# The mixer's step order of a hybrid decoder block, written out as a table

## The chip, the cores and the metric

One core of one Trainium2 chip. The metric is the device time of one execution in microseconds (us), the median over the runs shown; lower is better. Engines: TensorE (PE; its weight loads are PEld), VectorE (DVE), ScalarE (ACT), GpSimd (POOL) and SyncE (SP), which issues the transfers here. Each engine works its own queue in order, and the engines meet only at semaphores.

## What is computed

A decoder block over 2048 tokens of width 1024, in float32, with three parts:

```python
proj = rmsnorm(x) @ w_in               # q, k, v, g, z and two conv halves
o_gla = rmsnorm(gla_chunked(q, k, v, log_sigmoid(z @ w_gate_up + b) / 16)) * silu(g)   # 4 heads
u = c_in * sigmoid(c_gate)             # then a causal depthwise conv of 31 taps, 512 channels
o_conv = silu(channel_group_norm(conv(u)))
h = x + concat(o_gla, o_conv) @ w_out
h = h + square(relu(rmsnorm(h) @ w_mlp_in)) @ w_mlp_out
out = rmsnorm(h)
```

Everything but the last two lines is called the mixer here, the rest the MLP. Both kernels compute the same.

## The kernel before

The mixer works in four blocks of 512 tokens (b = 0 to 3). Precise products are made of three passes (`three_products`, L69: high times high, high times low, low times high), so that a weight tile is split into a rounded high part by ScalarE (L968) and a low part by GpSimd (L832) when it is new, stored to `w_kept` and loaded from there for later blocks (L616). A weight step ("unit") is one such tile of 512 columns and 12 matmuls of 128x512. Four tiles are on chip at a time (`SLOTS`), so that a load waits until the unit four places back is used.

The steps of one block, as PE sees them: `z` (the low-rank gate input), `qk_a`/`qk` 0 to 3 (q and k; the `_a` is the first half of the sum), `gate` 0 and 1 (L1635), `v` 0 to 7, `g_a`/`g` 0 to 3, then four transposes `x_tr` of the next block's normed tokens (L1488), 16 `out` units (the output projection of the block before, L1699 to L1701, in two halves of eight), and `conv_gate`/`conv_in` 0 to 3 for the next block. Between them stand small steps of other parts:

- The GLA recurrence, per chunk c of 128 tokens: `gla_expo` (DVE, L1406 to L1408, 15 differences of the cumulated decay into `fac`), `gla_factors` (ACT, exponentials, L1145 to L1147), `gla_decayed` in three parts (POOL, products into `ke` and `qe`, L861 to L921), `gla_heads` (ACT, L1155), `gla_scores` in four parts (PE, L1742 and L1746), each followed by `gla_select` (DVE, two masked copies into `probs`, L1431 or L1422), and `gla_out` (PE L1766 to L1773, ACT copy L1168, DVE state update L1440). Part n+1 of the scores writes the bank that the select of part n reads, so PE waits for that select. All of a chunk's scores free what `gla_decayed` of the next chunk writes.
- `decay` (DVE, a scan, L1372) needs both `gate` steps and ScalarE's logarithm; `gla_expo` 0 needs `decay`.
- The depthwise convolution: 124 taps a block, each one DVE instruction of 128x512 (L1248), in two pairs of channel tiles with 62 taps each (`taps`, pair, first, count). A pair needs `conv_in` of its tiles (DVE product L1347, which also frees the bank for the next `conv_in_a`).
- `cn_mean`, `cn_var`, `cn_rstd`, `cn_silu`, `cn_mixed` norm the convolution's output, and `gn_square`, `gn_sum`, `gn_rstd`, `gn_mixed` that of the recurrence; `v_done` (ACT, L1125) empties the banks of `v`.
- `x_load`, `x_sq`, `x_norm` bring the next tokens; `res_load` (SP, L679), `out_done` (DVE, L1389) and `store` (SP) add the residual and write h.

One list, PROGRAM, holds all steps, and every engine runs through it and takes its own instructions (`run`). So the place of a step sets its order on each engine that has a part in it, SP's and POOL's queues too. Before, the list is made by a planner: `block_steps` lays down the PE steps in a fixed order and puts the others where a due time, counted in weight units, falls (`gla_events` and the tables `CN0`, `CN0_MIX`, `CN1`, `GLA_AT`); `add_taps` then puts so many taps ahead of each DVE step as the numbers of TAP_PLAN say, and completes a pair where `conv_in` or `cn_mean` needs it. `last_steps` writes the way into the MLP by hand: `x_tr` of b = 4, the four `up0` products, and the last 16 `out` units.

```python
    for step, b in steps:
        name = step[0]
        if on_dve(step, b):
            emit(plan.pop(0) if plan else 0)
```

The MLP (from about 890 us on) is a loop over 16 groups of 256 hidden columns for each half of the tokens and isn't touched.

Of the kernel before, what the change touches and what calls it, by code (L numbers as in the profile page):

```python
# [87 lines left out]
def take_units():

    unit = 0  # L90

    def take(name, arg, n):
        nonlocal unit
        unit += n
        return (name, arg, unit - n, n)

    def column(name, j):
        return [take(name + "_a", j, 1), take(name, j, 1)]

    return take, column  # L100


def gla_events(b):

    events = [(8, ("gla_expo", 0)), (9.5, ("gla_factors", 0))] + [(10 + 1.3 * i, ("gla_decayed", 0, i)) for i in range(3)]
    start, period = GLA_AT.get(b, (15.6, 7.4))
    for c in range(TT):
        o = start + period * c
        if c + 1 < TT:
            events += [(o + 0.1, ("gla_expo", c + 1))]  # L110
        events += [(max(o - 1, 16), ("gla_heads", c))]
        for part in range(PARTS):
            events += [(o + 0.8 + PART_GAP * part, ("gla_scores", c, part)), (o + 0.8 + PART_GAP * part, ("gla_select", c, part))]
        if c + 1 < TT:
            events += [(o + 1.6, ("gla_factors", c + 1))]
            events += [(o + 2.6 + 1.2 * i, ("gla_decayed", c + 1, i)) for i in range(3)]
        events += [(o + 0.8 + PART_GAP * PARTS + 0.4, ("gla_out", c))]
    o = events[-1][0]
    if b < NB - 1:
        events += [(o + 1, ("gn_square",)), (o + 2.6, ("gn_sum", 0)), (o + 3.6, ("gn_sum", 1)), (o + 4.6, ("gn_rstd",))]  # L120
    return [(u, e, b) for u, e in events]


def block_steps(b, over):

    mix, nxt = b > 0, b < NB - 1
    kind = "start" if not mix else "body" if nxt else "end"
    take, column = take_units()
    steps = [] if nxt else [(("g2_load",), b)]
    steps += [(("x_load", t), b) for t in range(2 if mix else TT)]  # L130
    steps += [] if nxt else [(("m_load", i), b) for i in range(FT)]
    head = [("z",), *column("qk", 0), ("gate", 0), *column("qk", 1), ("gate", 1), *column("qk", 2),
            ("decay",), *column("qk", 3)]
    fill = head + [take("v", k, 1) for k in range(KT)]
    fill += [("v_done", 2 * 4 + KT - 1)]
    fill += [s for h in range(HEADS) for s in column("g", h)]
    fill += [("x_tr", 0), ("x_load", 2), ("x_tr", 1), ("x_load", 3)] if mix else [("x_tr", 0), ("x_tr", 1)]
    if mix:
        out0 = [take("out", (0, k), 1) for k in range(KT)]
        fill += out0[:1] + [("res_load", 0)] + out0[1:] + [("out_done", 0, out0[-1][2])]  # L140
    fill += [("x_tr", 2), ("x_tr", 3)]
    if mix:
        out1 = [take("out", (1, k), 1) for k in range(KT)]
        fill += [] if nxt else [("next_x", 0), ("next_x", 1)]
        fill += out1[:2] + [("store", 0)] + out1[2:3] + [("res_load", 1)] + out1[3:] + [("out_done", 1, out1[-1][2]), ("store", 1)]
    if nxt:
        for j in range(CT):
            fill += column("conv_gate", j) + column("conv_in", j)

    ev = over + gla_events(b)  # L150
    if mix:
        ev += [(0.8, ("cn_rstd", 1), b - 1), (1.6, ("cn_silu", 1), b - 1), (3.0, ("cn_mixed", 1), b - 1)]
        ev += [((13.2 + 1.2 * h if b == 1 else 4 + 1.4 * h), ("gn_mixed", h), b - 1) for h in range(HEADS)]
    ev += [(8 + i, ("x_sq", i), b) for i in range(2)] + [(12 + i, ("x_norm", i), b) for i in range(2)]
    late, scale = (26.6, 29) if mix else (12, 16)
    ev += [(late + i, ("x_sq", 2 + i), b) for i in range(2)] + [(scale + i, ("x_norm", 2 + i), b) for i in range(2)]
    if not nxt:
        ev += [(34.5 + i, ("x_sq", i), b + 1) for i in range(2)] + [(36.5 + i, ("x_norm", i), b + 1) for i in range(2)]
        ev += [(38 + 1.4 * i, ("m_split", i), b) for i in range(FT)]
    ev += [((20 if b == 1 else CN0[kind]) + u, (n, 0), b) for u, n in zip((0, 1.8, 3.3), ("cn_mean", "cn_var", "cn_rstd"))]  # L160
    ev += [(CN0[kind] + 8, ("cn_silu", 0), b), (CN0_MIX[kind], ("cn_mixed", 0), b)]
    if nxt:
        ev += [(CN1[kind] + u, (n, 1), b) for u, n in zip((0, 1.8), ("cn_mean", "cn_var"))]
    ev.sort(key=lambda e: e[0])

    at = 0
    for f in fill:
        while ev and len(f) == 4 and ev[0][0] <= at:
            steps.append(ev.pop(0)[1:])
        steps.append((("x_load", f[1]), b + 1) if f[0] == "next_x" else (f, b))  # L170
        if len(f) == 4:
            at += f[3]
    return steps, [(u - at, *e) for u, *e in ev]


CN0 = {"start": 28.5, "body": 17.5, "end": 17.5}
CN0_MIX = {"start": 38, "body": 40.2, "end": 40.2}
CN1 = {"start": 36.5, "body": 52.5}


def first_steps():

    s = []
    take, column = take_units()
    for j in range(CT):
        s += [(f, -1) for f in column("conv_gate", j) + column("conv_in", j)]
        s += [(("make_wz",), -1)] if j == 1 else []
    return s


def last_steps():

    take, column = take_units()
    out = [[(take("out", (half, k), 1), NB) for k in range(KT)] for half in range(2)]
    gla, mlp = NB - 1, NB

    def at(b, *steps):
        return [(step, b) for step in steps]

    s = at(gla, ("gn_square",)) + at(mlp, ("x_tr", 0), ("x_load", 2)) + at(gla, ("up0", 0), ("gn_sum", 0))  # L200
    s += at(mlp, ("x_tr", 1), ("x_load", 3)) + at(gla, ("gn_sum", 1), ("gn_rstd",), ("up0", 1))
    s += at(mlp, ("x_sq", 2)) + at(gla, ("cn_mean", 1)) + at(mlp, ("x_norm", 2), ("x_tr", 2), ("x_sq", 3))
    s += at(gla, ("cn_var", 1), ("gn_mixed", 0), ("gn_mixed", 1)) + at(mlp, ("x_norm", 3), ("x_tr", 3))
    s += at(gla, ("m_load", 2), ("m_load", 3), ("cn_rstd", 1), ("gn_mixed", 2), ("gn_mixed", 3), ("up0", 2))
# [7 lines left out]

def mixer_steps():

    steps, over = first_steps(), []
    for b in range(NB):
        more, over = block_steps(b, over)
        steps += more
# [1623 lines left out]
```

## Time and profile before

| | |
|---|---|
| median of 3 runs | 2349.61 us (2348.43 to 2351.4) |
| the profiled execution | 2348.33 us, of which its trace spans 2346.3 us |
| busy, share of the span | PE 96%, PEld 78%, DVE 51%, ACT 31%, POOL 28% |
| mean granted TensorE clock | 0.984 of full |
| the chain of waits, by engine | PE 74%, DVE 10%, POOL 2%, issue 1%, ACT 1%, DMA 1% |

A busy share is an average over stages: PE is at work without a break in the MLP, while in the mixer it waits now and then. The chain of waits goes back from the last instruction to what released it, and where it runs through DVE or POOL, that engine set the pace.

### The profile page before, as it was taken

How to read it: one execution, taken by the hardware profiler on the slowest of the kernel's cores; microseconds unless marked ns; L12 is line 12 of the kernel's file. 1: busy time of each engine (PE TensorE's matmuls, PEld its weight loads, DVE VectorE, ACT ScalarE, POOL GpSimd, SP SyncE). 2: the span in 40 equal slices, each digit the busy share in tenths (PEclk: the TensorE clock that was granted, in tenths of full speed). 3: DMA queues.
4: the chain of work that ended last, by engine and by line, in shares of the span. 5: the costliest groups of instructions: out<-in, count | busy, mean ns of one | idle time of the engine just before them, and what ended most of it. 6: DMA issues, size and time to landing. Idle time of an engine off the chain costs nothing.

```text
span 2346.3 us, 27675 instructions
## 1 busy us (share of the span) xinstructions
PE 2242.8 (96%) x10192; PEld 1831.6 (78%) x10192; DVE 1198.6 (51%) x1949; ACT 720.2 (31%) x1014; POOL 664.9 (28%) x697
## 2 busy tenths in 40 slices
PE   7989978998999999999999999999899999999998
PEld 6768767776877777888888888887788888888887
DVE  2898974389439942343433333436433343343345
ACT  3444553345235543112212212224221221221222
POOL 6443345142304332212221221224221222122122
...
GB/s 253 248 166 126 149 167 137 211 179 135 169 178 183 153 189 152 188 46 54 49 40 54 54 39 50 54 82 62 197 46 44 54 52 37 54 54 44 46 36 72
DMA packets 148518, 252.24 MB, mean 108 GB/s; under 512 B 9792, under 2 KB 91744, under 8 KB 148448
## 3 DMA queue, kind: packets, MB, share of 16 engines
...
## 4 chain that ended last, share of the span: by engine, by line
PE 74%; DVE 10%; POOL 2%; issue 1%; ACT 1%; DMA 1%; POOLq 0%; SPq 0%; ACTq 0%
PE acc L71 11%; PE acc L73 11%; PE acc L72 11%; PE acc L1566 10%; PE acc L1568 10%; PE acc L1567 10%; DVE acc L1248 5%; PE acc L1699 2%; PE acc L1701 2%; PE acc L1700 2%; PE acc L1742 2%; DVE fac L1406 1%; DVE fac L1407 1%; PE acc L1488 1%; PE acc L1718 1%
## 5 line engine op out<-in xcount | busy, mean ns | idle before, releaser
L1308 DVE TENSOR_TENSOR h_sb<-acc,h_sb 128x512 f32<-128x512 f32 x512 | 350.0, 690 | 274.8 <-PE acc L1568 268.4
L1566 PE MATMUL acc<-dn_hi,ff_hi 128*128 128x512 f32 x1024 | 400.1, 391 | 7.3 <-DVE h_sb L1308 5.5
L1567 PE MATMUL acc<-dn_lo,ff_hi 128*128 128x512 f32 x1024 | 399.1, 390 | 0.0
L1568 PE MATMUL acc<-dn_hi,ff_lo 128*128 128x512 f32 x1024 | 399.1, 390 | 0.0
L1326 DVE TENSOR_TENSOR relu<-relu 128x512 f32<-128x512 f32 x124 | 85.8, 692 | 463.4 <-ACT relu L1048 463.4
L884 POOL TENSOR_TENSOR up_lo<-raw_a,up_hi 128x1024 fp32r<-128x1024 f32 x62 | 149.3, 2431 | 584.5 <-ACT up_hi L1022 584.5
L1248 DVE SCALAR_TENSOR_TENSOR acc<-u_sb,cw_col,acc 128x512 f32<-128x512 f32 x464 | 312.0, 748 | 0.1
L884 POOL TENSOR_TENSOR dn_lo<-raw_b,dn_hi 128x1024 fp32r<-128x1024 f32 x62 | 147.2, 2396 | 456.0 <-ACT dn_hi L1022 456.0
L1566 PEld LDWEIGHTS acc<-dn_hi,ff_hi 128*128 128x128 f32 x1024 | 192.8, 188 | 47.9 <-DVE h_sb L1308 5.9
L1022 ACT ACTIVATE dn_hi<-raw_b 128x1024 fp32r<-128x1024 f32 x62 | 62.3, 1051 | 527.6 <-PE acc L1568 527.6
L1568 PEld LDWEIGHTS acc<-dn_hi,ff_lo 128*128 128x128 f32 x1024 | 192.7, 188 | 40.1
L1567 PEld LDWEIGHTS acc<-dn_lo,ff_hi 128*128 128x128 f32 x1024 | 192.8, 188 | 39.8
L71 PE MATMUL acc<-xT_hi,wt 128*128 128x512 f32 x512 | 213.8, 418 | 7.5 <-ACT v_sb L1125 4.7
L71 PE MATMUL acc<-xT_hi,up_hi 128*128 128x512 f32 x512 | 199.8, 390 | 3.2 <-DVE hT_lo L1280 3.2
L71 PE MATMUL acc<-hT_hi,up_hi 128*128 128x512 f32 x512 | 200.1, 391 | 1.5 <-DVE hT_lo L1267 1.5
L72 PE MATMUL acc<-xT_lo,wt 128*128 128x512 f32 x512 | 201.3, 393 | 0.0
L73 PE MATMUL acc<-xT_hi,wt 128*128 128x512 f32 x512 | 201.3, 393 | 0.0
L1048 ACT ACTIVATE relu<-acc 128x512 f32<-128x512 f32 x124 | 74.1, 598 | 413.3 <-PE acc L73 413.3
L73 PE MATMUL acc<-hT_hi,up_lo 128*128 128x512 f32 x512 | 199.9, 390 | 0.0
L72 PE MATMUL acc<-hT_lo,up_hi 128*128 128x512 f32 x512 | 199.9, 390 | 0.0
L72 PE MATMUL acc<-xT_lo,up_hi 128*128 128x512 f32 x512 | 199.2, 389 | 0.0
L73 PE MATMUL acc<-xT_hi,up_lo 128*128 128x512 f32 x512 | 199.2, 389 | 0.0
...
## 6 DMA issues: line engine op xcount, KB each, us to landing
wt<-w_kept SPq DMA_DIRECT2D x168, 512.0 KB, 3.3
raw_a<-in_w_mlp_in SPq DMA_DIRECT2D x64, 512.0 KB, 4.3
raw_b<-in_w_mlp_out SPq DMA_DIRECT2D x62, 512.0 KB, 3.5
w_kept<-wt SPq DMA_DIRECT2D x56, 512.0 KB, 4.9
...
h_sb<-h_dram SPq DMA_DIRECT2D x16, 512.0 KB, 8.9
out_h<-h_sb SPq DMA_DIRECT2D x16, 512.0 KB, 2.6
...
```

Source lines behind the costliest of these rows:

```text
L71: nc.tensor.matmul(out, w_hi, x_hi, start=first, stop=False)
L72: nc.tensor.matmul(out, w_hi, x_lo, start=False, stop=False)
L73: return nc.tensor.matmul(out, w_lo, x_hi, start=False, stop=last)
L884: nc.gpsimd.tensor_tensor(m_lo[i], raw[i], m_hi[i].bitcast(F32), ALU.subtract).then_inc(m_lo_ok, 1)
L1022: nc.scalar.activation(m_hi[i], raw[i], ACT.Copy).then_inc(m_hi_ok, 1)
L1048: nc.scalar.activation(relu[:, i, :], ps[:, i, :], ACT.Relu).then_inc(relu_ok, 1)
L1248: nc.vector.scalar_tensor_tensor(out=y_sb[:, j, :] if k == TAPS - 1 else bank, in0=u_sb[:, j, k:k + BLK], scalar=cw_col[:, j, k:k + 1], in ...
L1308: nc.vector.tensor_tensor(h_tile[t][:, c], ps[:, 4 + n % 4, :], h_tile[t][:, c], ALU.add).then_inc(add_ok, 1)
L1326: nc.vector.tensor_tensor(relu[:, i, :], relu[:, i, :], relu[:, i, :], ALU.mult).then_inc(sqr_ok, 1)
L1566: nc.tensor.matmul(o, ff_hi[:, i, r], m_hi[FT + i][:, c], start=(i == 0), stop=False)
L1567: nc.tensor.matmul(o, ff_hi[:, i, r], m_lo[FT + i][:, c], start=False, stop=False)
L1568: ins = nc.tensor.matmul(o, ff_lo[:, i, r], m_hi[FT + i][:, c], start=False, stop=(i == FT - 1))
```

## The change

PROGRAM is no longer planned. A literal table, ORDER, lists block, name and arguments of each step, taps included, and `mixer_steps` only numbers the weight units. The planner's functions and tables go. What an engine does in a step, the semaphores, the banks and the tiles are as before, and so are the order of the weight units and every step but the taps in number and kind (the 496 taps are cut into other groups, 755 entries before and 759 after).

```diff
-DVE_STEPS = (...)
-PART_GAP = 1.1
-GLA_AT = {0: (15.6, 6.9), NB - 1: (15.6, 6.6)}
-def take_units(): ...
-def gla_events(b): ...
-def block_steps(b, over): ...
-CN0 = ...
-def first_steps(): ...
-def last_steps(): ...
-def on_dve(step, b): ...
-def add_taps(steps): ...
-TAP_PLAN = [...]
+ORDER = [
...
+    (-1, "conv_gate", 1), (-1, "conv_in_a", 1), (0, "taps", 0, 0, 1), (-1, "conv_in", 1), (-1, "conv_gate_a", 2),
+    (-1, "conv_gate", 2), (0, "taps", 0, 1, 15), (-1, "make_wz"), (0, "x_load", 0), (-1, "conv_in_a", 2),
...
+    (0, "taps", 0, 16, 17), (-1, "conv_in", 3), (0, "z"), (0, "qk_a", 0), (0, "qk", 0), (0, "taps", 0, 33, 11),
...
+    (0, "x_sq", 2), (0, "v", 4), (0, "v_done", 15), (0, "gla_heads", 0), (0, "gla_decayed", 0, 2), (0, "x_sq", 3),
...
+    (1, "gla_decayed", 0, 2), (1, "gla_factors", 0), (1, "v", 6), (1, "gla_heads", 0), (0, "gn_mixed", 0),
...
+    (1, "gla_expo", 2), (1, "g", 2), (1, "g_a", 3), (1, "g", 3), (1, "x_tr", 0), (1, "gla_scores", 1, 0),
+    (1, "taps", 1, 55, 1), (1, "x_tr", 1), (1, "gla_select", 1, 0), (1, "x_load", 2), (1, "gla_select", 1, 1),
+    (1, "gla_select", 1, 2), (1, "x_load", 3), (1, "res_load", 0), (1, "out", 0, 0), (1, "cn_rstd", 0),
+    (1, "gla_scores", 1, 1), (1, "out", 0, 1), (1, "gla_decayed", 2, 0), (1, "gla_factors", 2),
+    (1, "gla_scores", 1, 2), (1, "gla_scores", 1, 3), (1, "x_sq", 2), (1, "x_sq", 3), (1, "gla_select", 1, 3),
...
+    (1, "out_done", 0, 31), (1, "gla_decayed", 2, 2), (1, "out", 0, 5), (1, "out", 0, 6), (1, "gla_heads", 2),
...
+    (1, "gla_select", 2, 1), (1, "gla_expo", 3), (1, "out", 1, 2), (1, "gla_scores", 2, 3), (1, "out", 1, 3),
...
+    (1, "conv_in", 1), (1, "conv_gate_a", 2), (2, "taps", 0, 0, 14), (1, "gn_rstd"), (1, "conv_gate", 2),
+    (1, "cn_var", 1), (2, "x_load", 0), (1, "conv_in_a", 2), (2, "taps", 0, 14, 3), (1, "conv_in", 2),
+    (1, "conv_gate_a", 3), (1, "conv_gate", 3), (1, "cn_rstd", 1), (1, "conv_in_a", 3), (1, "cn_silu", 1),
+    (2, "taps", 0, 17, 14), (1, "conv_in", 3), (2, "z"), (2, "qk_a", 0), (2, "qk", 0), (1, "gn_mixed", 0),
...
+    (2, "conv_in_a", 2), (3, "m_load", 0), (3, "taps", 0, 1, 28), (2, "conv_in", 2), (2, "cn_var", 1),
...
+    (3, "gn_square"), (4, "x_sq", 2), (3, "m_load", 2), (3, "m_split", 1), (3, "m_load", 3), (4, "x_norm", 2),
...
+]
 def mixer_steps():
+    steps, units = [], {}
+    for b, name, *args in ORDER:
+        if name in WEIGHT_STEPS:
+            n = units.get(b, 0)
+            units[b] = n + 1
+            steps.append(((name, args[0] if len(args) == 1 else tuple(args), n, 1), b))
+        else:
+            steps.append(((name, *args), b))
+    return steps
...
-        PROGRAM = add_taps(mixer_steps())
+        PROGRAM = mixer_steps()
```

Taps of a block that stand ahead of the last `conv_in` that feeds it, from there to `gla_expo` 0, and from there to the first `gla_select`, counted in both lists:

| block | taps ahead of `conv_in` 3, before / after | from it to `gla_expo` 0 | from it to `gla_select` 0, 0 |
|---|---|---|---|
| 0 | 2 / 33 | 48 / 25 | 77 / 49 |
| 1 | 30 / 32 | 46 / 41 | 74 / 64 |
| 2 | 6 / 31 | 40 / 22 | 63 / 48 |
| 3 | 6 / 33 | 40 / 17 | 63 / 41 |

In block 1, `gla_expo` 2 stood between the two first `x_tr` and `gla_select` 1, 0 and `gla_expo` 3 right ahead of `out_done` 0; now they stand ahead of `x_tr` 0 and behind `gla_select` 2, 1.

## Rows read from the trace of the kernel before

**Rows 1.** The page, first part: busy time of PE and its weight loads.
```profile
PE 2242.8 (96%) x10192; PEld 1831.6 (78%) x10192; DVE 1198.6 (51%) x1949; ACT 720.2 (31%) x1014; POOL 664.9 (28%) x697
```

**Rows 2.** Windows by stage: width, then each engine's busy time, granted clock, DMA share.
```profile
22.60:234.70 212.10, 198.53 (x933) 159.03 (x934) 160.34 (x297) 93.41 (x134) 100.71 (x141) 0.98 0.59 198
234.70:477.00 242.30, 216.21 (x1029) 172.52 (x1028) 147.22 (x266) 106.28 (x149) 80.86 (x112) 0.95 0.49 165
477.00:697.00 220.00, 207.00 (x983) 165.54 (x982) 151.37 (x279) 89.41 (x120) 60.62 (x96) 0.96 0.49 163
697.00:859.00 162.00, 151.86 (x778) 122.85 (x777) 142.67 (x259) 75.37 (x102) 65.50 (x104) 0.99 0.56 189
859.00:905.00 46.00, 40.22 (x157) 29.44 (x156) 20.84 (x30) 31.79 (x50) 12.83 (x14) 0.89 0.19 69
905.00:2346.30 1441.30, 1421.06 (x6289) 1175.96 (x6287) 565.03 (x809) 311.42 (x439) 333.06 (x198) 1.00 0.21 67
```

**Rows 3.** Waits of PE, 22 to 905 us: total us, times, longest.
```profile
PE acc L1742 <- DVE probs L1431: 22.5, 7, 5.2
PE acc L1488 <- DVE res_sb L1389: 13.8, 2, 10.2
PE acc L71 <- ACT v_sb L1125: 4.7, 1, 4.7
...
PE acc L1657 <- ACT k_sb L1115: 3.5, 4, 2.1
```

**Rows 4.** Windows around the start of block 2, same columns.
```profile
434.00:477.00 43.00, 43.00 (x190) 32.92 (x189) 11.82 (x22) 17.11 (x24) 0.00 (x0) 1.00 0.47 155
477.00:540.00 63.00, 57.47 (x249) 43.93 (x248) 62.79 (x109) 33.45 (x44) 27.10 (x35) 0.98 0.53 176
```

**Rows 5.** Timeline of DVE, block 2: start, us, engine, line, operation.
```profile
477.74 10.62 DVE L1248 SCALAR_TENSOR_TENSOR acc<-u_sb,cw_col,acc 128x512 f32<-128x512 f32 x16
...
505.40 5.77 DVE L1372 TENSOR_TENSOR_SCAN cum<-cum,sig 128x128 f32<-128x128 f32 x8
...
538.62 0.91 DVE L1431 COPY_PREDICATED probs<-lvl_mask,acc 128x256 f32<-128x256 int32 x2
```

**Rows 6.** Timeline of PE, block 2, at the second part of the scores.
```profile
539.58 1.65 PE L1742 MATMUL acc<-qe_head,ke 128*128 128x128 f32 x6 [4.04 <-DVE probs L1431]
```

**Rows 7.** Timeline of PE, block 0: matmuls of 512 columns at two paces.
```profile
127.32 0.63 PE L73 MATMUL acc<-xT_hi,wt 128*128 128x512 f32 x1
127.75 0.63 PE L71 MATMUL acc<-xT_hi,wt 128*128 128x512 f32 x1
...
134.67 0.40 PE L71 MATMUL acc<-xT_hi,wt 128*128 128x512 f32 x1
134.90 0.39 PE L72 MATMUL acc<-xT_lo,wt 128*128 128x512 f32 x1
```

**Rows 8.** Timeline of ACT, block 0: a weight split, later the heads.
```profile
125.14 0.63 ACT L968 ACTIVATE wt<-w_raw 128x512 fp32r<-128x512 f32 x1 [3.07 <-DMA w_raw<-in_w_in]
...
127.58 1.92 ACT L1155 ACTIVATE qe_head<-qe 64x896 f32<-64x896 f32 x2
```

**Rows 9.** Timeline of DVE, block 1: `gla_expo` 3 and `out_done` 0.
```profile
376.64 1.33 DVE L1406 TENSOR_TENSOR fac<-cum 128x128 f32<-128x128 f32 x1 [2.23 <-POOL qe L921]
...
379.17 0.28 DVE L1406 TENSOR_TENSOR fac<-cum 128x128 f32<-128x128 f32 x1
379.37 1.34 DVE L1407 TENSOR_TENSOR fac<-cum 128x128 f32<-128x128 f32 x1
...
384.17 2.48 DVE L1389 TENSOR_TENSOR res_sb<-acc,res_sb 128x512 f32<-128x512 f32 x4
```

**Rows 10.** Timeline of PE, block 1, at `x_tr` 2.
```profile
385.61 1.73 PE L1488 MATMUL acc<-ident,x_nat 128*128 128x128 f32 x7 [10.23 <-DVE res_sb L1389]
```

**Rows 11.** DMA issues: size of each, median us from issue to landing.
```profile
wt<-w_kept SPq DMA_DIRECT2D x168, 512.0 KB, 3.3
```

**Rows 12.** Timeline of POOL, block 1, beside rows 9.
```profile
379.29 1.28 POOL L832 TENSOR_TENSOR wt<-w_raw,wt 128x512 fp32r<-128x512 f32 x1 [0.19 <-ACT wt L968]
```

More of the change, by code:

```diff
@@ L81 @@
 WEIGHT_STEPS = COLUMNS + COLUMN_HALVES + ("v", "out")
-DVE_STEPS = ("make_wz", "conv_in", "gate", "decay", "gla_expo", "gla_select", "gla_out", "x_norm", "x_tr", "out_done",
-             "cn_mean", "gn_rstd", "cn_rstd", "cn_mixed", "ff0")
-PART_GAP = 1.1
-GLA_AT = {0: (15.6, 6.9), NB - 1: (15.6, 6.6)}
[L88 to L100, printed above, removed]
@@ L103, in gla_events @@
[L103 to L121, printed above, removed]
@@ L124, in block_steps @@
[L124 to L173, printed above, removed]
@@ L176 @@
[L176 to L204, printed above, removed]
-    s += at(gla, ("cn_silu", 1), ("cn_mixed", 1), ("up0", 3)) + at(mlp, ("res_load", 0))
-    s += out[0][:2] + at(gla, ("ff0", 0), ("ff0", 1)) + out[0][2:4] + at(mlp, ("res_load", 1))
-    s += at(gla, ("ff0", 2), ("ff0", 3)) + out[0][4:6] + at(gla, ("m_split", 2), ("m_split", 3)) + out[0][6:]
-    s += at(mlp, ("out_done", 0, out[0][-1][0][2])) + out[1][:4] + at(mlp, ("store", 0), ("late_load",)) + out[1][4:]
-    s += at(mlp, ("out_done", 1, out[1][-1][0][2]), ("store", 1))
-    return s
@@ L213, in mixer_steps @@
-def mixer_steps():
[L215 to L218, printed above, removed]
-    return steps + [tuple(e) for _, *e in over] + last_steps()
-def on_dve(step, b):
-    name = step[0]
-    if name in ("cn_rstd", "cn_mixed"):
-        return b == NB - 1 and step[1] == 1
-    return name in DVE_STEPS
-def add_taps(steps):
-    out = []
-    todo = [(m, p, i) for m in range(NB) for p in range(2) for i in range(PAIR_TAPS)]
-    plan = list(TAP_PLAN)
-    def emit(n):
-        while n > 0:
-            m, p, i = todo[0]
-            k = min(n, PAIR_TAPS - i)
-            out.append((("taps", p, i, k), m))
-            del todo[:k]
-            n -= k
-    for step, b in steps:
-        name = step[0]
-        if on_dve(step, b):
-            emit(plan.pop(0) if plan else 0)
-        if name == "conv_in" and b >= 0:
-            emit(sum(1 for m, p, i in todo if m < b or m == b and p <= step[1] // 2))
-        if name == "cn_mean":
-            emit(sum(1 for m, p, i in todo if m < b or m == b and p <= step[1]))
-        out.append((step, b))
-    assert not todo
-    return out
```

130 lines of the change are left out of this document (128 added, 2 removed), and 7 rows, old and new, of the table TAP_PLAN.

## Prediction

> **What bounds the kernel.** I read the busy shares first: PE is at work for 2242.8 of 2346.3 us, so all that any order can win is 103.5 us of idle PE, and a little clock [rows 1]. The windows by stage say where that is. After 905 us the loop runs, which the change doesn't touch. The mixer's stages are idle for width less busy: 13.6, 26.1, 13.0, 10.1 and 5.8 us, 68.6 in all [rows 2]. The first 22.6 us are startup and stay. The waits of PE name the releasers: 22.5 us for VectorE's selects, 13.8 for its residual sums, 4.7 for the copy of v, 3.5 for that of k [rows 3]. VectorE has only half its time filled, so the order matters: in 434 to 477 us it works 11.8 of 43 us while PE is full, and in the next 63 us it works all but 0.2 and PE loses 5.5 [rows 4].
>
> **Prices.** A tap costs 10.62/16 = 0.664 us in a run of taps, `decay` 5.8, a select pair 0.9 [rows 5]. Twelve matmuls, 0.227 us apart at full clock (134.67 to 134.90), make 2.7 us a weight unit [rows 7]. The profiled execution took 2348.3 us, 1.3 under the median of 2349.6; savings come off both.
>
> **Clock.** After a stall, matmuls start 0.43 us apart instead of 0.23, thus at 1.2 instead of 2.4 GHz [rows 7]. I count some 50 of them in six stretches behind stalls from 126 to 892 us: 50 x 0.2 = 10 us, of which 2.4 in block 0, 4.0 in block 1, 1.6 in block 2, 2 at the end. The Trainium skill (TensorE: Matmul & The Clock Gate, Terms) prices a throttled clock at its time times the share of pulses withheld; with the granted clocks of the stages that would be 32 us, and a kernel without the stalls would come out some 12 us lower than my sum. Most of that lower clock lies inside the idle time, which is counted already, so I keep 10.
>
> **Part 1: taps go where VectorE was idle.** 33, 32, 31 and 33 taps stand ahead of `conv_in` 3 instead of 2, 30, 6 and 6, and the path to `gla_select` 0, 0 holds 28, 10, 15 and 22 fewer. In block 2 VectorE runs without a break from 477.7 to the select at 538.6, and PE waits 4.04 us for it [rows 5, 6]; 15 taps less are 10.0 us, so that stall goes, and its twins in blocks 0, 1 and 3 (22 taps, 14.6 us) too. The next to be late is the chain `gla_factors`, `gla_decayed`, `gla_heads`; it hangs on `gla_expo` 0, which comes earlier by 23, 5, 18 and 23 taps, so it isn't late in blocks 2 and 3. Price of the new places: PE waits at `conv_in_a` and `qk_a` for VectorE's product behind the taps. Block 2: 14 taps (9.3) stand against two units and the 16 matmuls of `z` (2 x 2.7 + 3.6 = 9.0), nothing worth a term. Block 3: 28 taps (18.6) and two products, each taken as a select (1.8), 20.4 us, against six units (16.3) and six matmuls of the norms (some 3.3) on PE, 19.6: 0.8 us. Where GpSimd or a late start holds VectorE up, this cover is gone and each microsecond counts in full; the ends are 0 and 5 a block, for 14 taps are nearly two units of work more than there is room for if VectorE is late by one.
>
> **Part 2: block 1's second half.** `gla_expo` 3 waited for GpSimd until 376.6 and took until 384.2, `out_done` behind it; `x_tr` 2 stood 10.23 us [rows 9, 10]. With it behind `gla_select` 2, 1, `out_done` starts on its `out_pe` and the stall goes. With `gla_expo` 2 ahead of `x_tr` 0, so does a stall of 5.2 at the scores, one of the seven [rows 3]. What remains: `gla_scores` 1, 2 and 1, 3 now stand side by side, as do 3, 0 and 3, 1, and each pair makes PE wait for a select, 0.9 plus handover, 1.4 each. `x_norm`, `x_load`, the stores: bounded by nothing and 1 us; I take nothing, since the same transfers run under the same units.
>
> **Part 3: block 0.** `v_done` moves ahead of the splits of `v` 5 to 7 on ScalarE; before, a split waited 3.07 us for a load, and the copy of v behind it cost PE 4.7 [rows 3, 8]. Now the first scores come ahead of `g_a`, and wait for `gla_heads`: the last copy of v, taken as the split's 0.63, and the heads' 1.92 behind `v` 7 make 2.6 us, where POOL's `gla_decayed` is ready by then; if it is not, up to 5 [rows 8]. The `xT_lo` and select stalls go with the taps.
>
> **Part 4: SP's queue.** `res_load` 0 stands ahead of `out` 0, 0 (block 1) and of `g_a` 2 (block 2), and waits there for GpSimd's `cn_rstd`; weight loads queue behind it. A load has three units, 8.2 us, before it is needed, and lands in 3.3 [rows 11]: 4.9 us of slack. I find a delay of about 3. Cost 0, bound 0 to 5 for each of three blocks. GpSimd's splits behind `gla_decayed` 3, 0 get through 1 to 2 us ahead of PE by the same count.
>
> **Part 5: the way into the MLP.** `m_split` 1 now stands behind `x_sq` 2, which waits for a load, and `gn_sum` 1 behind both: 2.4 us new. `x_tr` 2 no longer waits, 2.0 less. The others stay. I take 0, between -3 and +5.
>
> **Sum**, idle and slow clock, before to after:
>
> - block 0: 13.6 + 2.4 to 5.4 (2.6 heads, 1.0 clock, 1.8 small): 10.6
> - block 1: 26.1 + 4.0 to 9.4 (2.0 k copy and 1.6 clock stay, 1.5 `out` and gate, 2.8 score pairs, 1.5 small): 20.7
> - block 2: 13.0 + 1.6 to 3.5 (a pair 1.4, `x_tr` 0.5, selects 1.6): 11.1
> - block 3: 10.1 to 5.5 (1.8 at `gla_out` stays, `conv_in_a` 0.8, selects 2.9): 4.6
> - end: 5.8 + 2 to the same: 0
>
> Together 47.0. A count on paper finds the waits that it looks for; the before has 26 stalls in 68.6 us, 2.6 each, and I put in three that I don't see: 7.9. That leaves 39.1, and 2349.6 - 39.1 = 2310.5; I say 2311. Nothing removed could give more than 68.6 + 10 = 78.6, thus 2271.
>
> **Rivals.** *Half of it* (0.17): blocks 0 and 1, where GpSimd also splits new weights, turn their stalls into others of the same size, and only blocks 2 and 3 gain: 11.1 + 4.6 = 15.7, 2334. For it: `gate` 0 of block 1 sits behind 24 taps and a `gla_out`, and PE is then held by `gate_min`. Against it: block 1 loses its two largest stalls whatever the taps do.
>
> *Nothing* (0.08): each stall is replaced, within 0.2% (4.7 us, about what a measurement here can tell from no change). The 26 stalls would have to be replaced by as much; 2350. For it: a step can only be early on one engine by being late for another. Against it: VectorE has 31 us of the 43 free where the taps go [rows 4].
>
> *Slower, the shared access to memory* (0.11). `gla_expo`'s differences take 0.28 us, but 1.34 while GpSimd subtracts [rows 9, 12]; a whole `gla_expo` with four of them took 7.5 us (376.64 to 384.17) against 14 x 0.2 + 0.4 = 3.2. The new places put `gla_expo` 0 and 1 beside `gn_mixed` and `gla_decayed`. If half of the 16, on the path, are stretched by 4.3, that is 34 us, and what part 1 gains (about 32 of the 47) goes too, so 2350 - 15 + 34 = 2369. It decides once a block's stretch passes the 10 us by which its selects come earlier. Against it: GpSimd is busy for 28% of the span only [rows 1], and the new places of `gla_expo` 2 and 3 take these two out of GpSimd's splits. The Trainium skill (SBUF — State Buffer, Who interferes with whom) states that a VectorE instruction with two SBUF inputs is shut out by a GpSimd instruction that reads SBUF, and that one with a single SBUF input isn't; by that rule the taps, one of whose inputs is in PSUM, never stretch. The trace agrees for both kinds.
>
> That the change does nothing can't be: the order of most small steps differs.
>
> **Numbers.** The forecast holds with 0.64, from 2290 (all but 19 us of the 78.6) to 2328. *Half of it* carries the range up to 2340; that leaves out the other two. Faster 0.81, same 0.08, slower 0.11.
>
> **What would show it.** In the profile after: VectorE busy some 20 us more in the 43 us ahead of the last `conv_in` of blocks 2 and 3; no PE wait over 2 us for `probs`; none for `res_sb` at `x_tr` 2; a new wait for `qe_head` of 2 to 3 us in block 0, and of 1.4 us at three pairs of scores; the loop's 1441 us unchanged. I am wrong if PE waits for `u_sb` in the conv stage by more than 3 us a block, for `wt` loads, or for the heads in blocks 1 to 3.

## The result and the profile after

The changed kernel takes **2277.82 us** (median of 4 runs, 2274.8 to 2278.47) against 2349.02 for the one before beside it (4 runs): a ratio of 0.9694, 95% interval 0.9677 to 0.9711, thus 71.2 us or 3% faster. The prediction said faster, but 2311, with a range from 2290 to 2340. The direction is right, but the measured time lies 33 us below the forecast and 12 us below the range.

The page after, first part:

```profile
PE 2225.5 (98%) x10192; PEld 1820.1 (80%) x10192; DVE 1186.5 (52%) x1949; ACT 713.8 (31%) x1011; POOL 660.7 (29%) x697
```

Beside [rows 1]: the same 10192 matmuls, and PE is not only idle for 52.7 us less (50.8 of 2276.3 instead of 103.5), it is also *busy* for 17.3 us less. DVE has the same 1949 instructions and is busy for 12.1 us less. Two engines do the same work faster, which an order alone doesn't seem able to do; both differences are explained below.

Windows of after, cut at the fourth `u_sb` product of each block (the `conv_in` 3 of the prediction) and at the first matmul of the MLP; columns as in [rows 2]:

```profile
22.60:70.62 48.02, 48.02 (x203) 38.72 (x204) 26.53 (x41) 14.69 (x24) 30.57 (x40) 1.00 0.86 295
70.62:223.55 152.93, 148.70 (x740) 119.84 (x738) 136.80 (x257) 74.61 (x105) 66.56 (x99) 0.99 0.56 188
223.55:436.54 212.99, 209.65 (x1032) 166.35 (x1031) 153.70 (x289) 115.55 (x162) 89.21 (x118) 1.00 0.55 187
436.54:636.13 199.59, 198.04 (x974) 159.34 (x973) 148.69 (x280) 82.23 (x114) 54.88 (x94) 1.00 0.53 181
636.13:816.06 179.93, 171.98 (x866) 137.50 (x865) 135.56 (x250) 91.41 (x130) 67.14 (x111) 0.99 0.51 174
816.06:2276.30 1460.24, 1441.29 (x6352) 1192.09 (x6352) 574.14 (x820) 322.80 (x457) 341.12 (x204) 0.99 0.21 67
```

The same for before, where its windows in [rows 2] ended elsewhere:

```profile
696.94:888.28 191.34, 175.42 (x869) 138.66 (x867) 156.49 (x277) 96.21 (x134) 72.81 (x114) 0.98 0.51 171
888.28:2346.30 1458.02, 1437.78 (x6352) 1189.62 (x6352) 572.10 (x820) 322.37 (x457) 338.59 (x203) 1.00 0.21 67
```

The mixer ends at 816.06 instead of 888.28, 72.2 us earlier; what follows is untouched and takes 2.2 us longer. Of the 72.2, 51.5 are idle PE (68.6 to 17.1, width less busy over the mixer's windows) and 20.7 are PE's busy time.

PE's waits after, 22 to 860 us (total us, times, longest), to be held against [rows 3]:

```profile
PE acc L1715 <- DVE probs L1404: 3.4, 3, 1.3
PE acc L1461 <- DVE x_nat L1229: 2.5, 2, 1.4
PE acc L1715 <- ACT qe_head L1128: 2.5, 1, 2.5
PE acc L1739 <- DVE probs L1395: 2.4, 3, 1.7
```

The selects went from 22.5 us to 3.4, the residual sum (13.8) and the copy of v (4.7) from the list altogether.

### The profile page after: what moved, and what is told of

It is laid out like the page before. It is cut to its first block, busy times and chain, and to the rows that moved or that the text cites. A ratio compares the mean times of both kernels' runs of the same rounds, so it can differ in the third digit from the quotient of the medians.

```text
span 2276.3 us, 27673 instructions
## 1 busy us (share of the span) xinstructions
PE 2225.5 (98%) x10192; PEld 1820.1 (80%) x10192; DVE 1186.5 (52%) x1949; ACT 713.8 (31%) x1011; POOL 660.7 (29%) x697
## 4 chain that ended last, share of the span: by engine, by line
PE 92%; DVE 5%; ACT 2%; issue 1%; DMA 0%; POOL 0%; SPq 0%; POOLq 0%; ACTq 0%
PE acc L71 15%; PE acc L72 15%; PE acc L73 15%; PE acc L1539 10%; PE acc L1540 10%; PE acc L1541 10%; PE acc L1672 2%; PE acc L1674 2%; PE acc L1673 2%; PE acc L1715 2%; PE acc L1630 1%; PE acc L1632 1%; PE acc L1631 1%; DVE acc L1221 1%; PE acc L1461 1%; PE acc L1739 1%
## 5 line engine op out<-in xcount | busy, mean ns | idle before, releaser
L73 PE MATMUL acc<-xT_hi,wt 128*128 128x512 f32 x512 | 200.9, 392 | 0.0
```

What stands on the lines that cost most here:

```text
L73: return nc.tensor.matmul(out, w_lo, x_hi, start=False, stop=last)
```

## The experiments

All kernels are written as a literal table like the new one, so "the order of before" is what the planner gave, put down as a table. Here are the mixer's stages of each run's trace, cut as above (width, and in brackets the idle PE in it), and the median. Each kernel was timed beside the kernel before, whose own median lay between 2346.5 and 2349.0. The intervals stand with each run and are ratios to that kernel. Where a run is held against the new table's 2277.8, two measurements at different times are compared, so differences of 2 or 3 us there say nothing. The trace is of one execution; that of `decay_back` took 2299.5 us, 7 us more than its median, which its readings below have to bear.

| kernel | start and block 0 | block 1 | block 2 | block 3 and way into the MLP | median |
|---|---|---|---|---|---|
| before | 212.1 (13.6) | 242.4 (26.1) | 219.8 (13.0) | 191.3 (15.9) | 2349.0 |
| taps_only | 219.2 (17.0) | 237.6 (23.0) | 227.9 (19.6) | 201.9 (20.3) | 2371.9 |
| steps_only | 219.0 (17.8) | 224.7 (12.7) | 208.9 (5.7) | 205.9 (28.8) | 2344.0 |
| taps_decay | 216.3 (13.6) | 238.1 (21.5) | 217.4 (13.0) | 192.8 (17.6) | 2346.1 |
| gn_only | 212.4 (13.5) | 238.3 (22.5) | 210.4 (7.2) | 187.9 (11.8) | 2332.3 |
| named4 | 214.2 (13.8) | 228.8 (14.2) | 216.6 (11.8) | 192.0 (15.4) | 2334.9 |
| named4_conv | 202.3 (5.5) | 229.4 (15.0) | 207.8 (6.3) | 189.6 (16.0) | 2311.9 |
| after | 200.9 (4.2) | 213.0 (3.3) | 199.6 (1.6) | 179.9 (8.0) | 2277.8 |

**The two halves of the change.** `taps_only` takes the order of before and puts every tap ahead of the VectorE step that it has behind it in the new table; `steps_only` is the reverse. In block 2, as an example:

```diff
 (2, "qk", 0),
-(2, "taps", 0, 6, 16), (2, "gate", 0), (2, "qk_a", 1), (2, "qk", 1), (2, "taps", 0, 22, 9), (2, "gate", 1),
+(2, "taps", 0, 31, 14), (2, "gate", 0), (2, "qk_a", 1), (2, "qk", 1), (2, "taps", 0, 45, 1), (2, "gate", 1),
 (2, "qk_a", 2), (2, "qk", 2),
-(2, "taps", 0, 31, 15), (2, "decay"),
+(2, "taps", 0, 46, 5), (2, "decay"),
```

> The order of before with every tap moved to where the new table has it (ahead of the same VectorE step); all other steps stay. The prediction put some 32 of its 47 us down to the taps. Theory A (a stall costs its idle time, and matmuls of 512 columns at half rate are all that the clock adds): 2349 less about 32, thus near 2317, and PE's busy time falls by no more than 6 us. Theory B (the lower clock behind each stall reaches the narrow matmuls too and costs some 0.4 us for each us of idle time): near 2304, with PE's busy time down by 12 or more. Rival C (taps alone change nothing without the steps, since gla_expo still comes late): 2335 or more.

> The new table's order of all other steps, with the taps ahead of the same VectorE steps as before the change (10 taps deferred to the conv_in that they need, 16 of block 3 drawn ahead of a cn_mean). If the two parts add up, as the prediction's sum takes them to, its gain and that of the run with the taps alone make 71 us together; theory A gives 15 us of them here, 2334; theory B 22, 2327. If the gains need each other, the two together stay clearly below 71 us; if they overlap, they come out above it.

The taps alone are **slower**: 2371.9 us, ratio 1.0095 (1.0070 to 1.0119). The steps alone give almost nothing: 2344.0, 0.9982 (0.9969 to 0.9996). 24 us lost and 4 won make 71 won when put together. This refutes the prediction's view that 32 of the 47 us belong to the taps, and theories A and B. Rival C had the reason, and its 2335 or more holds, but it spoke of no change, not of 24 us lost. (One wait of 11.3 us for `y_sb` in block 3 of `steps_only` comes from 16 taps that this mixture has to put ahead of a `cn_mean`. The steps alone are thus judged too low here: without that wait they would win some 15 us, an estimate from 4.1 + 11.3 that wasn't tested. Even so the halves don't add up to 71.)

The trace of `taps_only` says why. VectorE in block 2, ahead of the scan `decay`, and ScalarE at the same time, then ScalarE's logarithm in the same block of the kernel before:

```profile
496.75 3.38 DVE L1218 SCALAR_TENSOR_TENSOR acc<-u_sb,cw_col,acc 128x512 f32<-128x512 f32 x5
506.49 5.82 DVE L1342 TENSOR_TENSOR_SCAN cum<-cum,sig 128x128 f32<-128x128 f32 x8 [6.36 <-ACT sig L1077]
```

```profile
501.02 0.60 ACT L1085 ACTIVATE k_sb<-acc 128x512 f32<-128x512 f32 x1 [4.97 <-PE acc L73]
501.64 1.28 ACT L1075 ACT_TABLE_LOAD   x1
502.93 1.06 ACT L1075 ACTIVATE sig<-sig 128x1024 f32<-128x1024 f32 x1
504.01 1.28 ACT L1077 ACT_TABLE_LOAD   x1
505.30 1.15 ACT L1077 ACTIVATE sig<-sig,one_col 128x1024 f32<-128x1024 f32 x1
```

```profile
504.00 1.15 ACT L1107 ACTIVATE sig<-sig,one_col 128x1024 f32<-128x1024 f32 x1
```

VectorE has done its taps at 500.1 and waits 6.4 us for ScalarE's logarithm. ScalarE was free for five of them, but the step `decay` stands behind `qk` 2, and so its logarithm behind the copy of the result of `qk` 2, which PE has only then. The scan begins at 506.5, 1.1 us later than before [rows 5], in a block whose fourth `u_sb` product begins 2.3 us later (479.4 against 477.1). So it comes 1.2 us earlier in its block, where 20 taps less on the way from there to it would have made 13. Before, the taps had only filled this wait: the logarithm ended at 505.15 and the scan began at 505.40. The taps taken away ahead of it bought next to no time, and 9 instead of 3 now stand right ahead of the select: the wait at the scores grew from 4.0 to 8.2 us.

**decay.** One step moved per block, in the old order and in the new one:

```diff
+(2, "decay"),
 (2, "qk_a", 2), (2, "qk", 2),
-(2, "decay"),
```

> The run with the taps alone, and the step decay of each block ahead of the next weight unit where the new table has it (before qk_a 2, in block 1 before qk 2), two units earlier. Theory D: with the taps alone VectorE idles 6.4 us in block 2 ahead of decay, because ScalarE's logarithm for it stands in ScalarE's queue behind the copies of qk 2; so gla_expo 0 is no earlier than before, and the taps moved behind it make the select late. With decay moved this idle goes in every block, the waits for the selects of chunk 0 (8.2 and 5.5 us in blocks 2 and 3) shrink to under 3 us, and the time falls from 2372 to 2350 or below. Rival E (decay isn't what is missing, the other steps are): less than 8 us come back, 2364 or more.

> The new table with decay alone moved back behind qk 2 in all four blocks. Theory D: VectorE waits some 6 us for the logarithm in each block, and the selects of chunk 0 get late by what slack doesn't take: 15 to 30 us in all, so 2293 to 2308, most of it in blocks 2 and 3. Rival E: the slack of the new order covers it, and the time is within 5 us of 2278.

With `decay` two units earlier (one in block 1), the taps' run falls from 2371.9 to 2346.1, 0.9985 (0.9975 to 0.9996), and the waits in blocks 2 and 3 from 8.2 and 5.6 to 2.1 and 2.4, as theory D had it. Moved back in the new table, the step costs 14.5 us: 2292.3, 0.9758 (0.9742 to 0.9775), somewhat below the 15 to 30 expected, and in its trace, whose mixer is 21.2 us wider, more in blocks 0 and 1 (7.6 and 5.2 us) than in 2 and 3 (4.7 and 3.8), against what was expected. What PE waits for there is ScalarE's copy of k, which now stands behind the logarithm and its two table loads. PE in blocks 0 and 1, and ScalarE in block 0:

```profile
101.54 0.50 PE L1630 MATMUL acc<-wt,xT_hi 128*128 128x512 f32 x1 [2.93 <-ACT k_sb L1088]
270.51 0.79 PE L1630 MATMUL acc<-wt,xT_hi 128*128 128x512 f32 x1 [3.16 <-ACT k_sb L1088]
```

```profile
95.15 1.28 ACT L1078 ACT_TABLE_LOAD   x1
96.44 1.06 ACT L1078 ACTIVATE sig<-sig 128x1024 f32<-128x1024 f32 x1
97.52 1.28 ACT L1080 ACT_TABLE_LOAD   x1
98.82 1.15 ACT L1080 ACTIVATE sig<-sig,one_col 128x1024 f32<-128x1024 f32 x1
...
100.91 0.57 ACT L1088 ACTIVATE k_sb<-acc 128x512 f32<-128x512 f32 x1
```

The same place thus costs in two ways: late for VectorE, and late for PE.

**gla_expo 2 and 3 of block 1.**

```diff
+(1, "gla_expo", 2),
 (1, "g", 2), (1, "g_a", 3), (1, "g", 3), (1, "x_tr", 0), (1, "x_load", 2), (1, "x_tr", 1), (1, "x_load", 3),
-(1, "gla_expo", 2),
...
-(1, "gla_expo", 3),
 (1, "out", 0, 7), (1, "out_done", 0, 31),
...
 (1, "gla_scores", 2, 1), (1, "gla_select", 2, 1),
+(1, "gla_expo", 3),
```

> The order of before with two moves in block 1: gla_expo 2 ahead of g 2, and gla_expo 3 behind gla_select 2, 1. Two stalls of PE, of 10.2 and 5.2 us, should go. Theory A: 15.4 us less or somewhat under it, so 2334 to 2337. Theory B: the clock comes back with them, 15.4 x 1.4 = 21.6, so near 2328, with PE's busy time 4 us or more below before's. Rival: the select or the residual sum stays late by its taps, and less than 10 us come back.

> The new table with gla_expo 2 and 3 of block 1 moved back to where they stood (ahead of gla_select 1, 0 and of out_done 0). If the prediction's part 2 is right, the stall at x_tr 2 returns with about 10 us and that at the scores with up to 5: idle 15, with the clock's 0.4 for each 21, thus 2293 to 2299. If the two moves are worth in the new order what they were in the old one (11.5 us measured), 2289. If the new order no longer has GpSimd in their way, less than 5 us, 2283.

Alone the two moves give 11 to 12 us: 2336.6, 0.9947 (0.9929 to 0.9965). Both stalls go (0.5 us is left of the 10.2), but PE now comes to `out` 1, 0 before VectorE has taken the low half of the transposed tokens out of the banks that this unit writes:

```profile
377.37 0.80 PE L1671 MATMUL acc<-wt,mix_hi 128*128 128x512 f32 x1 [3.46 <-DVE xT_lo L1239]
```

Taken back from the new table they cost 8.5: 2286.3, 0.9735 (0.9719 to 0.9752), between the 2283 and the 2289 put forward. The stalls that return are 4.93 and 2.34 us, not 10.2 and 5.2. So the moves are right, and worth 8.5 to 12 of the 15.4 us booked in part 2: in the old order a new wait takes part of it, in the new one the stalls would be half as long anyway.

**GpSimd beside VectorE.** DVE's busy time is 12 us lower after, and the trace shows where: the scan `decay` takes 5.77 us in block 2 before [rows 5] and 2.63 after, `gla_expo` 0 behind it 6.6 and 3.2. Before, GpSimd works through `gn_mixed` at that moment. (Nearly as much comes from block 1, where `gla_expo` 1 and 3 fall from 7.2 and 7.5 to 3.2 each; in block 3 of after the scan still takes 3.7 and `gla_expo` 0 5.3.) Moving `gn_mixed` ahead in blocks 2 and 3 of the order of before tests it:

```diff
 (2, "qk", 0),
+(1, "gn_mixed", 0), (1, "gn_mixed", 1),
 (2, "taps", 0, 6, 16), (2, "gate", 0), (2, "qk_a", 1),
+(1, "gn_mixed", 2),
...
-(1, "gn_mixed", 0),
 (2, "qk_a", 2), (2, "qk", 2), (2, "taps", 0, 31, 15), (2, "decay"),
-(1, "gn_mixed", 1),
 (2, "qk_a", 3),
-(1, "gn_mixed", 2),
...
```

> The order of before, with only the four gn_mixed steps of blocks 2 and 3 moved ahead (0 and 1 behind qk 0, 2 behind qk_a 1, 3 behind v_done), so that GpSimd's products aren't beside decay and gla_expo 0. In before decay takes 5.8 and gla_expo 0 6.6 us in these blocks; alone they take 2.6 and 3.2. Theory S (two VectorE inputs from SBUF beside GpSimd make them long): decay and gla_expo 0 fall to 2.6 and 3.2, the select of chunk 0 comes 6.6 us earlier, and the waits of 1.2 and 4.0 us in each of the two blocks go: 10.5 us of idle, with the clock 14.7, so 2334. Rival: they stay long, or the path is set elsewhere, and less than 3 us come back.

> The new table with the gn_mixed steps of blocks 2 and 3 moved back to where they stood (0 behind gate 1, the others behind decay). Theory S: decay and gla_expo 0 become 5.8 and 6.6 us long in block 2 (2.6 and 3.2 now), 6.6 us together, of which VectorE's idle time behind them takes 3.5; in block 3, where they are long already (3.7 and 5.3), up to 3 us more. On PE 3 to 6 us, with the clock 4 to 8: 2282 to 2286. Rival: VectorE's slack in the new order takes all of it, 2278 within 2.

`gn_only` came out as worked out: 2332.3 us, 0.9944 (0.9928 to 0.9961), 14.2 us less. VectorE in block 2:

```profile
501.77 2.63 DVE L1344 TENSOR_TENSOR_SCAN cum<-cum,sig 128x128 f32<-128x128 f32 x8
508.81 0.76 DVE L1220 SCALAR_TENSOR_TENSOR acc<-u_sb,cw_col,acc 128x512 f32<-128x512 f32 x1
```

The same eight scans take 2.63 instead of 5.77 us. Taps don't stretch beside GpSimd's products; nine of them in block 2 of before, with GpSimd at work from 491.46 on:

```profile
488.94 6.01 DVE L1248 SCALAR_TENSOR_TENSOR acc<-u_sb,cw_col,acc 128x512 f32<-128x512 f32 x9
```

```profile
491.46 2.52 POOL L934 TENSOR_TENSOR mix_lo<-y_sb,mix_hi 128x512 fp32r<-128x512 f32 x2 [5.48 <-ACT mix_hi L1197]
493.95 2.53 POOL L941 TENSOR_TENSOR o_sb<-o_sb,silu_g 128x512 f32<-128x512 f32 x2
```

0.668 us each, against 0.664 in [rows 5]. In the new table (`gn_back`) the move back stretches the scan of block 2 to 8.93 us beside six products of GpSimd (`gla_expo` 0 stays at 3.25), and yet the time is 2278.2, 0.9718 (0.9701 to 0.9734), no different from the new table's: the rival's value, not the 2282 to 2286 of theory S. Its mixer is 3.3 us longer in the trace, half of the 6.3 us that VectorE lost in block 2, which would mean that the new order has room for the rest. The Trainium skill (SBUF — State Buffer, Who interferes with whom) states that the port pair which VectorE shares with GpSimd is an exclusive lock; the traces agree with it, for the scan too, both of whose inputs are in SBUF.

**Taps ahead of conv_in 3.**

```diff
-(2, "taps", 0, 6, 8) ... (2, "taps", 0, 14, 3) ... (2, "taps", 0, 17, 14), (1, "conv_in", 3),
+(1, "conv_in", 3), (2, "taps", 0, 6, 25),
```

> The new table with 25 taps of block 2 and 27 of block 3 moved from ahead of conv_in 3 to right behind it, which leaves 6 ahead as in the kernel before. The prediction's part 1: 16.6 and 17.9 us more of VectorE's work then stand on the path to gla_select 0, 0, of which its idle time there (about 5 and 9 us) takes a part, so that PE waits some 11 and 9 us more: 20 us of idle, 2298; with the clock's 0.4 for each, 28 us, 2306. Rival: the taps ahead of conv_in 3 delay it as much as they help, less than 8 us, 2286 or less.

2302.4 us, 0.9821 (0.9805 to 0.9837), 24.6 more than the new table, between the two theories. PE's waits:

```profile
460.93 2.07 PE L1607 MATMUL acc<-sig,w_up 32*128 32x512 f32 x2 [11.25 <-DVE cum L1335]
672.26 2.07 PE L1607 MATMUL acc<-sig,w_up 32*128 32x512 f32 x2 [12.74 <-DVE cum L1335]
```

The size is about as expected, the place isn't: PE stops at `gate` 1, whose bank `gate` 0's `gate_min` on VectorE has to empty, and no longer at the selects. In the new order the gates, not the selects, are the first to suffer when VectorE is late.

**Do the stages stand by themselves?** Two splices at `z` of block 2, and a table built up from all moves named so far.

```diff
+[new table, up to (1, "conv_in", 3)]       in splice_ab
 (2, "z"),
+[new table, from here on]                  in splice_ba
```

> The new table up to z of block 2, and the order of before from there on. If the stages are independent, the gain is that of the stages up to there as the two traces have it: 40.6 us (mixer stages 454.5 us before, 413.9 after), and nothing behind, so 2308. If what stands early in the first part helps or hurts the second, it is off that by more than 3 us.

> The order of before up to z of block 2, and the new table from there on, the counterpart to the splice that took 2305.8. If the stages are independent, it has the gain of the last two of them alone: 411.1 us before, 379.5 after, 31.6, so 2317; and the two splices' gains (40.7 and this) make 72. If the taps that the new order has ahead of conv_in 3 are needed from before the cut (25 of them are missing here), up to 12 us less.

`splice_ab` takes 2305.8, 0.9827 (0.9810 to 0.9843), 40.7 us less, where 40.6 was expected: blocks 0 and 1 keep their own gain. `splice_ba` takes 2336.0, 0.9945 (0.9926 to 0.9965), 10.9 less instead of 31.6. Its blocks 2 and 3 lack 17 of their 31.6 us, all of it in block 2, where the 25 taps aren't done yet and the wait at `gate` 1 is to the digit the one of `preconv_back`:

```profile
509.15 2.07 PE L1607 MATMUL acc<-sig,w_up 32*128 32x512 f32 x2 [11.25 <-DVE cum L1335]
```

Some 5 us more are missing in blocks 0 and 1 of the trace, 3.5 of them in block 1, whose steps stand in the order of before: there `gla_expo` 1, with GpSimd at work beside it, took 9.3 us (292.71 to 302.03) instead of 7.2, and the wait at the scores behind it 8.8 instead of 5.0. The order is the same, so this is how the engines happened to meet. So the stages are independent but for the taps that are done ahead, within such a scatter.

`named4` is the order of before with the edits of `taps_decay`, `gn_only` and `expo23_only` together; `named4_conv` adds the rest of one stage:

```diff
+(b, "conv_gate_a", 0) ... (b + 1, "z")     all steps in the new table's order, b = 0 to 2
```

> The order of before with the four things named so far as in the new table: all taps, decay, the gn_mixed steps of blocks 2 and 3, and gla_expo 2 and 3 of block 1. If effects simply add (taps 24 slower, decay 26, gn_mixed 14 and gla_expo 11.5 faster), 2349 - 27.5 = 2321. If the parts need each other and these four are the change, it comes near 2278, under 2290. If the new waits for VectorE's products u_sb in the conv stage, 13 us with the taps alone, stay because the small steps between the taps there are still in the old order, it stays above 2310.

> The run before this one, with all steps from conv_gate_a 0 to z of the next block, in blocks 0 to 2, in the new table's order too. If the order in the conv stage is what the taps lacked, the waits for u_sb go, 13 us of idle, with the clock 18 us below the run before this one. Rival: the conv stage's own order doesn't matter, within 5 us of it.

`named4` comes to 2334.9, 0.9949 (0.9930 to 0.9967). Added up, the four singles would have given 2321. The taps' price is still in it, in the conv stage of block 2:

```profile
671.99 0.79 PE L71 MATMUL acc<-xT_hi,wt 128*128 128x512 f32 x1 [5.44 <-DVE u_sb L1317]
```

With all small steps of the conv stage in the new order, every wait for `u_sb` is gone, and the time is 2311.9, 0.9849 (0.9831 to 0.9867), 23 us below `named4`, where 18 had been expected. 34 us above the changed kernel remain: `named4_conv` still has 25.8 us more idle time than after, most of it from the first scores of a block to its last `out` unit, in waits of 0.5 to 4.2 us for ten different releasers. Which single moves remove them wasn't tried.

**The slow clock.** PE's busy time fell by 20.7 us in the mixer. Groups of PE's instructions, before and then after, with equal counts (busy us, mean ns; idle):

```profile
L1742 PE MATMUL acc<-qe_head,ke 128*128 128x128 f32 x448 | 67.0, 294 | 26.2 <-DVE probs L1431 22.5 <-ACT qe_head L1155 3.7
L1488 PE MATMUL acc<-ident,x_nat 128*128 128x128 f32 x160 | 26.7, 328 | 29.6 <-DVE x_nat L1256 13.8 <-DVE res_sb L1389 13.8 <-ACT silu_g L1131 1.9
```

```profile
L1715 PE MATMUL acc<-qe_head,ke 128*128 128x128 f32 x448 | 60.8, 276 | 5.9 <-DVE probs L1404 3.4 <-ACT qe_head L1128 2.5
L1461 PE MATMUL acc<-ident,x_nat 128*128 128x128 f32 x160 | 22.9, 291 | 12.1 <-DVE x_nat L1229 12.1
```

The narrow matmuls right behind a stall are slow as well as the wide ones: 6.2 us came back in the scores and 3.8 in the transposes. In block 1 of before eight of them take 1.87 us behind a stall, and the next eight, at full clock, 1.05:

```profile
308.56 1.87 PE L1742 MATMUL acc<-qe_head,ke 128*128 128x128 f32 x8 [5.02 <-DVE probs L1431]
313.93 1.05 PE L1742 MATMUL acc<-qe_head,ke 128*128 128x128 f32 x8
```

The granted clock says how much it is. In the mixer it stood at half, 1.2 GHz, for 60.6 us before and 7.6 us after, and PE was busy in 46.7 and 6.8 of them. Half of that busy time, 23.4 and 3.4, is what the low clock cost: 20.0 us less, of the 20.7 measured.

What a stall adds was measured twice in the new table, with taps drawn ahead of a select:

```diff
-(2, "taps", 1, 17, 7), (2, "gla_select", 0, 2), ... (2, "taps", 1, 24, 4), ... (2, "taps", 1, 28, 9),
+(2, "taps", 1, 17, 20), (2, "gla_select", 0, 2),              in stall_back
+(2, "taps", 1, 17, 12), (2, "gla_select", 0, 2),              in four_stalls, and 3, 2 and 6 taps elsewhere
```

> The new table with 13 taps of block 2 (24 to 36 of its second pair) drawn ahead of gla_select 0, 2, so that PE waits 13 x 0.664 = 8.6 us longer at gla_scores 0, 3; VectorE's work and all later places stay. Against the new table's 2277.8, theory A: 8.6 less up to 1.5 that later waits give back, thus 2285 to 2287, PE's busy time the same within 1 us. Theory B: the clock behind the stall adds about 0.4 x 8.6 = 3.4 us in PE's busy time, near 2289 to 2290.

> The new table with four smaller groups of taps drawn ahead of a select each: 5 and 3 in block 2 (gla_select 0, 2 and 1, 2), 2 in block 1 (1, 2), 6 in block 3 (0, 2), so that PE gets four stalls some 1 to 4 us longer, 7 to 8 us of idle in all, about as much as the single stall of 7.1 us of the run stall_back added (which cost 10.6). If the slow clock behind a stall goes by its idle time (0.4 for each us), this one costs as much, 10 to 11, so 2288 to 2289. If it goes by the number of stalls (1.5 to 3 us of PE's busy time each, however long), four cost 6 us or more on top of the idle time, 2292 or more.

`stall_back` takes 2288.4, 0.9739 (0.9717 to 0.9760), 10.6 more than the new table, nearer to theory B (2289 to 2290) than to A (2285 to 2287). The stall and two of the wide matmuls behind it:

```profile
508.33 1.23 PE L1714 MATMUL acc<-qe_head,ke 128*128 128x128 f32 x4 [7.12 <-DVE probs L1403]
511.49 0.63 PE L71 MATMUL acc<-xT_hi,wt 128*128 128x512 f32 x1
511.92 0.63 PE L72 MATMUL acc<-xT_lo,wt 128*128 128x512 f32 x1
```

They stand 0.43 us apart, 1.2 GHz. 7.0 us of idle brought 3.2 us of busy time. `four_stalls` doesn't decide its question: only two of the four stalls appeared (1.86 and 2.91 us; VectorE had room at the other two), its mixer is idle for 4.3 us more and busy for 1.0 us more, and at 2279.9, 0.9709 (0.9691 to 0.9726), it is within 2 us of the new table. Over the runs the busy time added for each us of idle was 0.46 in `stall_back`, 0.23 here, 0.14 in `preconv_back` (two long stalls, 24.0 and 3.4 us) and 0.71 in `decay_back` (12.4 and 8.8, in five stalls of 1.7 to 4.3). Most of it follows from the granted clock, as above: half of PE's busy time at 1.2 GHz, less the new table's 3.4, is 3.2, 1.7, 3.9 and 7.3 us, where 3.2, 1.0, 3.4 and 8.8 were measured. In `preconv_back` the clock stood at half for 30.7 us, but PE stood still for more than half of them, so that its long stalls cost little beside their idle time; in `decay_back` it was busy in 21.5 of 24.8. The differences of up to 1.5 us lie in the scatter of busy time, which in the loop, the same in all kernels, was 1436.9 to 1441.3. What makes the clock fall behind one stall and not behind another stays open.

**A version beyond.** The new table's three cleanest waits, taken away:

```diff
-(0, "gla_scores", 0, 0), (0, "gla_factors", 1), (0, "g_a", 0),
+(0, "gla_factors", 1), (0, "g_a", 0), (0, "gla_scores", 0, 0),
...
 (1, "gla_scores", 1, 3) with its select moved behind (1, "out", 0, 2), that of block 2 behind (2, "out", 0, 3)
```

> The new table with three of its remaining waits taken away: gla_scores 0, 0 of block 0 behind g_a 0 again (it waits 2.5 us for the heads), and gla_scores 1, 3 with its select one out unit later in blocks 1 and 2 (1.3 us each at score pairs). Each wait gone with its clock: 5.1 x 1.4 = 7, so 2271; if only idle comes back, 2273. If the waits come back at the next select or at gla_out 1, 2277 or more.

2277.7, 0.9696 (0.9680 to 0.9712), the same as the new table. All three waits went, and others of their size took their place:

```profile
126.02 0.79 PE L71 MATMUL acc<-xT_hi,wt 128*128 128x512 f32 x1 [3.20 <-POOL wt L805]
549.15 2.04 PE L1461 MATMUL acc<-ident,x_nat 128*128 128x128 f32 x14 [1.67 <-DVE res_sb L1362]
```

None of the runs was faster than the changed kernel beyond the uncertainty.

## Why the prediction's size was wrong, and where it was right

Right was the direction and its ground: the time is in the 68.6 us in which PE waits in the mixer, and the loop behind it stays. Wrong was the size, 39.1 us forecast and 71.2 measured, outside the whole range. The shortfall in the mixer is 72.2 - 39.1 = 33.1 us, and it splits into three terms of the sum:

| | forecast | measured | short by |
|---|---|---|---|
| idle PE removed | 41.6 (47.0 less 5.4 of clock) | 51.5 | 9.9 |
| slow clock removed | 5.4 | 20.7 | 15.3 |
| allowance for unseen waits | -7.9 | 0 | 7.9 |

- **The clock term failed**, and it is nearly half of the miss. "I count some 50 of them ... = 10 us" counted only matmuls of 512 columns at half rate, and the bound "nothing removed could give more than 68.6 + 10" rested on it. The narrow ones had as much to give by the instruction groups (6.2 and 3.8 us), and by the granted clock the slow clock cost 23.4 us before, not 10, so that the bound lay near 92. The Trainium skill's formula (TensorE: Matmul & The Clock Gate, Terms), which the prediction quoted as 32 us and set aside, was nearer: with the granted clocks of the stages after, 3.3 us remain by it, so it would have had 26 to 29 removed, where 20.7 were. The argument against it, that most of the low clock lies inside the idle time, is false: 13.9 of the 60.6 us at half clock were idle, less than a quarter.
- **The allowance** was for waits that the count wouldn't see. There were none: idle time by stage was 4.2, 3.3, 1.6 and 8.0 us after, against 4.4, 7.8, 3.5 and 11.3 forecast (block 3 with the end). Every stage came out at or below its count, most of all block 1, where no `k_sb` wait of 2.0 stayed, but one of 0.8.
- **Part 1's attribution failed.** "32 of the 47" for the taps alone: alone they cost 24. The step that fails is "it hangs on `gla_expo` 0, which comes earlier by 23, 5, 18 and 23 taps". Its chain ran through VectorE only, and left out that `decay` waits for ScalarE's logarithm, and so on where the step stands in ScalarE's queue. It also priced the taps' new places in block 3's conv stage at 0.8 us, which holds only with the conv stage's other steps in the new order; with the old ones it was 5.4. That the selects' waits went all the same was luck as far as the argument goes: the table moves these steps as well, which the prediction hadn't credited.
- **`decay` at 5.8 us** was taken as its own duration. 3.1 of it was GpSimd's share, as were 3.4 of `gla_expo` 0's 6.6. The prediction knew the mechanism, but booked it only as a danger; the new order takes it away in block 2 and in part in block 3 (3.7 and 5.3 us are left), and moving `gn_mixed` alone is worth 14 us in the old order.
- **Part 2** was over-counted: 8.5 to 12 us instead of 15.4. **Part 3** was right: a new wait for `qe_head` in block 0, 2.6 forecast and 2.49 measured. **Part 4**: no wait for a `wt` load is left over 0.3 us. **Part 5**, the way into the MLP, was put at nothing; its `x_nat` waits of 1.98 and 2.30 became one of 1.42, and no new one at `gn_sum`.

Of the signs named ahead: no wait for `probs` at a select over 2 us (longest 1.3), none for `res_sb`, pairs of scores with 1.29 and 1.28 us, two of the three forecast (1.4). VectorE ahead of the last `conv_in` of blocks 2 and 3:

```profile
393.50:436.50 43.00, 43.00 (x182) 31.74 (x181) 28.49 (x46) 26.40 (x33) 5.05 (x4) 1.00 0.48 164
593.10:636.10 43.00, 42.99 (x188) 32.32 (x188) 33.04 (x51) 19.43 (x27) 3.25 (x2) 1.00 0.52 176
```

28.5 and 33.0 us busy instead of 11.8 in both [rows 4, and the same for block 3], 17 and 21 more where 20 were forecast, and PE full in both.

The rival of the **shared access** had its mechanism shown and its sign wrong for this change. *Half of it* falls with `splice_ab`: blocks 0 and 1 alone give 40.7 us, most of any part, and block 1 alone 29.4. *Nothing* fits the steps alone (4 us won), but not the taps alone (24 lost).
